# Gate projections of the attention stage: two column chunks formed together as seven half-size products

## What is computed

```
pr = split(h @ w_in)            # gates are pr[11], pr[12], pr[13]
ga, gb, gc = (sigmoid(t) for t in pr[11:14])
y = ga * (o_a @ w_proj_a) + gb * (o_b @ w_proj_b) + gc * (o_c @ w_proj_c)
return y @ w_out
# o_c = softmax(q k^T / 8) v over 768 keys, 16 query heads in 8 pairs
```

## Time and profile before

| what | value |
|---|---|
| median of three executions | 2822.43 us |
| span of the profiled execution | 2814.1 us |
| median less span (start and end around it) | 8.3 us |
| PE busy | 2697.8 us, 96% |
| DVE busy | 1246.7 us, 44% |
| ACT busy | 523.0 us, 19% |
| attention stage, first scores to last values | 753.6 to 1176.2 us |

### The profile page before, as it was taken

One profiled execution on the slowest core, in us unless ns is written; L12 is line 12 of the kernel. 1 busy time (PEld: TensorE's weight loads), 2 busy tenths in 40 slices (PEclk: granted clock), 3 DMA queues, 4 the chain that ended last, 5 costly groups with the idle time before them and its releaser, 6 DMA issues.

```text
span 2814.1 us, 32083 instructions
## 1 busy us (share of the span) xinstructions
PE 2697.8 (96%) x12682; PEld 1796.7 (64%) x12682; DVE 1246.7 (44%) x2310; ACT 523.0 (19%) x870; POOL 171.2 (6%) x140
## 2 busy tenths in 40 slices
PE   7999999999899999999799999989999999999997
PEld 3688888887544444586344333334496877888886
DVE  4255656664444344535311111146573335654644
ACT  3122121222233233211100000022322113100001
POOL 1122211220000000132000000000000000000000
PEclk9999999999999999999899999999999999999999
DMA  9622111211111111225599999942102421233330
GB/s 346 212 60 57 54 52 45 60 30 38 38 53 53 45 53 49 79 75 183 231 409 409 409 409 409 409 154 64 42 1 83 125 77 46 78 87 90 90 90 30
DMA packets 327673, 374.57 MB, mean 133 GB/s; under 512 B 10033, under 2 KB 273030, under 8 KB 324230
## 3 DMA queue, kind: packets, MB, share of 16 engines
q1 hardware_dynamic: 327286, 371.93, 38.6%
q10 hardware_dynamic: 272, 1.05, 0.1%
HBM read 370.85 MB, written 2.10 MB: 133 GB/s over the span
## 4 chain that ended last, share of the span: by engine, by line
PE 91%; DVE 4%; DVEq 1%; DMA 1%; ACT 1%; issue 1%; SPq 0%; ACTq 0%
PE psum L1650 31%; PE psum L1952 12%; PE psum L1381 8%; PE psum L2108 6%; PE psum L720 3%; PE psum L1118 2%; PE psum L1837 2%; PE psum L815 2%; PE psum L728 2%; PE psum L2642 2%; PE psum L1878 2%; PE psum L705 2%; PE psum L1308 2%; PE psum L1360 2%; PE psum L1337 1%; PE psum L2724 1%
## 5 line engine op out<-in xcount | busy, mean ns | idle before, releaser
L1650 PE MATMUL psum<-arena 128*128 128x256 f32 x4144 | 907.9, 378 | 1.0 <-ACT arena L2740 0.5
L1650 PEld LDWEIGHTS psum<-arena 128*128 128x128 f32 x4144 | 779.2, 189 | 116.2 <-issue 5.3
L1952 PE MATMUL psum<-arena 128*64 128x512 f32 x1536 | 347.6, 597 | 3.0 <-issue 2.1
L1952 PEld LDWEIGHTS psum<-arena 128*64 128x64 f32 x1536 | 104.9, 136 | 217.5 <-issue 214.4
L1381 PE MATMUL psum<-arena 128*128 128x512 f32 x512 | 233.1, 597 | 0.0
L2108 PE MATMUL psum<-arena 128*128 128x512 f32 (+1 forms) x448 | 168.1, 532 | 0.0
L1682 DVE TENSOR_TENSOR arena<-psum,arena 128x256 f32<-128x256 f32 x66 | 28.0, 425 | 315.2 <-ACT arena L1695 192.6
L1381 PEld LDWEIGHTS psum<-arena 128*128 128x128 f32 x512 | 92.4, 189 | 104.1 <-issue 104.1
L1883 DVE SCALAR_TENSOR_TENSOR arena<-psum,arena 128x512 f32<-128x512 f32 x64 | 48.0, 750 | 246.4 <-PE psum L1878 245.8
L2108 PEld LDWEIGHTS psum<-arena 128*128 128x128 f32 x448 | 84.8, 190 | 80.8 <-issue 77.3
L1657 POOL TENSOR_TENSOR arena<-arena 128x512 f32<-128x512 f32 x34 | 48.2, 1418 | 1119.7 <-DMA arena<-in_w_in 653.3
(11 more groups left out here) (378 smaller groups left out, 3202.9 us busy)
## 6 DMA issues: line engine op xcount, KB each, us to landing
arena<-in_w_gate SPq DMA_DIRECT2D x64, 1024.0 KB, 18.3
arena<-in_w_up SPq DMA_DIRECT2D x64, 1024.0 KB, 16.2
arena<-in_w_down SPq DMA_DIRECT2D x64, 1024.0 KB, 18.0
arena<-in_w_in SPq DMA_DIRECT2D x120, 512.0 KB, 4.0
arena<-in_ada_w SPq DMA_DIRECT2D x24, 1024.0 KB, 7.4
arena<-in_w_up SPq DMA_DIRECT2D x32, 512.0 KB, 5.3
arena<-in_w_down SPq DMA_DIRECT2D x32, 512.0 KB, 4.8
arena<-in_w_out SPq DMA_DIRECT2D x16, 512.0 KB, 3.8
```

Source lines behind the costliest of these rows:

```text
L1650: mm = pe.matmul(psum[:, base + b, c * HALF:(c + 1) * HALF], w, v, start=(first and q == 0 and m in (0, 2, 3, 4)), stop=(last and q == KC ...
L1952: mm = pe.matmul(psum[64 * e:64 * e + 64, bank + n, :], tokens(e, 2 * q + k), w[:, k, 512 * n:512 * n + 512], start=(q == 0 and k == 0), s ...
```

## The change

The gates of two neighbouring chunks are formed together as a pair with seven half-size products. Pair q (0 to 7) is branch a for even q, branch b for odd q, and the chunks 2(q // 2) and 2(q // 2) + 1. Every attention pair q now has one gate pair and two projections:

- step t = 0: `pe_gate` phase 0 (products 0 and 1, bank 6) and phase 1 (product 4, bank 7);
- step t = 1: phase 2 (products 3 and 5, bank 6) and phase 3 (products 6 and 2, bank 7);
- steps t = 2 and 3: `pe_branch`, the projections of the two chunks, as before but into banks 6 and 7.

Each phase's results are taken out of PSUM by `act_gate_copy` and `dve_gate`; the sigmoid is formed once per pair over 1024 columns (`act_gate`, in step t = 2), and `dve_branch` multiplies and adds. `form_gate_sums` forms the four weight sums of the next pair on DVE in step t = 3. The units of a pair are now ordered query, gate, gate, projection, projection, in the same four places. Three waits of the merge stage name the new units and counts. The core of the diff:

```diff
-        def unit_of_fill(f):
-            q, r = f // 4, f % 4
-            return 5 + 5 * q + (r + 1 if r and q < PAIRS_Q - 1 else r)
+        def unit_of_fill(q, r):
+            return 5 + 5 * q + (q < PAIRS_Q - 1) + r
...
-            return 5 * q + 1 if q else Q0
+            return 5 * q if q else Q0
...
+        def form_gate_sums(eng, q):
+
+            for e in range(2):
+                ws.arrived(eng, "attn", 0, unit_of_fill(q, e))
...
+                done(eng, "attn", 0, unit_of_fill(q - 1, 1))
+            weight_sums(eng, *gate_weights(q), gate_sums(q), "gate_sums")
+
+        PHASES = [(0, 1), (4,), (3, 5), (6, 2)]
+
+        def pe_gate(pe, q, phase):
...
+            if phase == 0:
+                for e in range(2):
+                    ws.arrived(pe, "attn", 0, u + e)
+                if q == 0:
                     pe.wait_ge(sem("head_root"), HEADS)
+                else:
+                    pe.wait_ge(sem("branch_out"), 2 * q - 1)
+            if phase == 1:
+                pe.wait_ge(sem("gate_sums"), q + 1)
...
+                    pe.wait_ge(sem("branch_out"), 2 * q)
+            if phase >= 2:
+                pe.wait_ge(sem("gate_parts"), 4 * q + phase - 1)
+            for at_, m in enumerate(PHASES[phase]):
+                for j in range(KC // 2):
+                    e, o = 2 * j, 2 * j + 1
...
+                    mm = pe.matmul(psum[:, 6 + phase % 2, at_ * HALF:(at_ + 1) * HALF], w, v, start=(at_ == 0 and j == 0),
+                                   stop=(j == KC // 2 - 1), skip_group_check=True)
...
+        def act_gate(act, q):
+
+            m = m_gate
+            act.wait_ge(sem("gate_parts"), 4 * q + 4)
+            act.activation(m, m, ACT.Exp, scale=-1.0)
...
+        def pe_branch(pe, q, e, part):
...
+            if part == 0:
+                ws.arrived(pe, "attn", 0, u)
+                pe.wait_ge(sem("gate_parts"), 4 * q + 3 + e)
...
         def dve_attn(dve):
+            form_gate_sums(dve, 0)
             for s in range(NSTEP):
                 q, t = s // 4, s % 4
+                if t == 0 and q:
+                    dve_branch(dve, q - 1, 1)
+                if t == 1:
+                    dve_gate(dve, q, 1)
+                if t == 2:
+                    dve_gate(dve, q, 3)
                 dve_max(dve, s, 0)
                 dve_max(dve, s, 1)
                 dve_scale(dve, s, 0)
...
                 turned_copy(dve, s, 1)
-                if s and s % 2 == 0:
-                    dve_fill(dve, s - 1)
+                if t == 0:
+                    dve_gate(dve, q, 0)
+                if t == 1:
+                    dve_gate(dve, q, 2)
+                if t == 3:
+                    dve_branch(dve, q, 0)
+                    if q < PAIRS_Q - 1:
+                        form_gate_sums(dve, q + 1)
...
-                    done(pool, "attn", 0, unit_of_fill(4 * KC - 3))
+                    done(pool, "attn", 0, unit_of_fill(PAIRS_Q - 2, 3))
...
-            pe.wait_ge(sem("gate_out"), FILLED)
+            pe.wait_ge(sem("branch_out"), FILLED - 1)
```

More of the change, by code:

```diff
@@ L1055, in mixed_block_kernel @@
             sources[unit_of_query(q)] = w_in_at("aq", q)
[L1056 to L1058 removed]
+        for q in range(PAIRS_Q):
+            for e in range(2):
+                c = 2 * (q // 2) + e
+                sources[unit_of_fill(q, e)] = w_in_at("g" + "ab"[q % 2], c)
+                sources[unit_of_fill(q, 2 + e)] = lambda i, b=q % 2, c=c: w_proj[b][c]
         ws.phase("attn", 1, [(sources[n],) + unit_place(4 + n % 4) for n in range(len(sources))],
@@ L1077, in mixed_block_kernel @@
         a_q = [at.take(S)]
+        gate_a, gate_u = at.take(HALF), at.take(HALF)
         at = Carve(arena, EXTRA[0], HG_END)
         a_q.append(at.take(S))
-        m_gate = [at.take(S) for _ in range(2)]
+        m_gate = at.take(2 * S)
         late = [at.take(S) for _ in range(3)]
@@ new lines, in gate_sums @@
+        def gate_sums(q):
+            if q < 4:
+                kept = [yT[:, 5 + m, :].rearrange("p (k n) -> p k n", n=P) for m in range(3)]
+            else:
+                area = Carve(arena, HG_END + NT * 2 * P, HG_END + NT * 2 * P + 2 * T)
+                kept = [area.take(KC // 2, P) for _ in range(3)]
+            return kept + [gate_weights(q)[1].rearrange("p (k h) n -> p h k n", h=2)[:, 0]]
+        def form_gate_sums(eng, q):
+            for e in range(2):
+                ws.arrived(eng, "attn", 0, unit_of_fill(q, e))
+            if q == 0:
+                eng.wait_ge(sem("head_out"), HEADS + 1)
+            elif q == 4:
+                eng.wait_ge(sem("scores_1"), 16)
+            else:
+                done(eng, "attn", 0, unit_of_fill(q - 1, 1))
+            weight_sums(eng, *gate_weights(q), gate_sums(q), "gate_sums")
@@ new lines, in mixed_block_kernel @@
+        PHASES = [(0, 1), (4,), (3, 5), (6, 2)]
+        def pe_gate(pe, q, phase):
+            u = unit_of_fill(q, 0)
+            wa, wb = gate_weights(q)
+            sums = gate_sums(q)
+            x = HT[:, :, C:T]
+            if phase == 0:
+                for e in range(2):
+                    ws.arrived(pe, "attn", 0, u + e)
+                if q == 0:
+                    pe.wait_ge(sem("head_root"), HEADS)
+                else:
+                    pe.wait_ge(sem("branch_out"), 2 * q - 1)
+            if phase == 1:
+                pe.wait_ge(sem("gate_sums"), q + 1)
+                if q == 0:
@@ L1393, in sigmoid_gate, with dve_branch @@
             act.drain()
[L1394 to L1401, removed]
+            act.activation(m, m, ACT.Exp, scale=-1.0).then_inc(sem("gate_out"), 2)
+        def pe_branch(pe, q, e, part):
+            u = unit_of_fill(q, 2 + e)
+            x = (aT, bT)[q % 2]
+            if part == 0:
+                ws.arrived(pe, "attn", 0, u)
+                pe.wait_ge(sem("gate_parts"), 4 * q + 3 + e)
+            for k in range(4 * part, 4 * part + 4):
+                mm = pe.matmul(psum[:, 6 + e, :], ws.dst("attn", u)[:, k, :], x[:, k, :], start=(k == 0), stop=(k == KC - 1))
+            if part:
+                mm.then_inc(sem("weights_used"), 1)
+        def dve_branch(dve, q, e):
+            m, c = m_gate[:, e * S:e * S + S], 2 * (q // 2) + e
+            dve.wait_ge(sem("gate_out"), 2 * q + 2)
+            done(dve, "attn", 0, unit_of_fill(q, 2 + e))
+            dve.tensor_tensor(m if q % 2 else yT[:, c, :], m, psum[:, 6 + e, :], ALU.mult)
             dve.drain()
-            if not first:
+            if q % 2:
                 dve.tensor_tensor(yT[:, c, :], yT[:, c, :], m, ALU.add)
@@ L1406, in gated_branch, with pe_filler @@
             dve.sem_inc(sem("branch_out"), 1)
[L1408 to L1414, removed]
+        def pe_filler(pe, s, part):
+            q, r = s // 4, s % 4
+            if r < 2:
+                pe_gate(pe, q, 2 * r + part)
+            else:
+                pe_branch(pe, q, r - 2, part)
         def pe_attn(pe):
```

54 lines of the change are left out of this document (41 added, 13 removed).

## The result

Four executions of the changed kernel took 2802.54 to 2809.33 us, a median of 2805.44 us against 2822.61 us for four of the kernel before: a ratio of 0.9942 with a 95% interval of 0.9929 to 0.9954. Forecast were 2809.2 us in a range of 2805 to 2815. The change is faster by 17 us, 0.6%.

A forecast was written before the change was run, and what follows sets the result against it. PE work was taken to bound the attention stage. Removed columns gave -13.2 us, all other terms 0: span 2814.1 to 2800.9, plus 8.3 to the median, 2809.2 us; range 2805 to 2815, the forecast's own 2806 to 2812.

The forecast's parts named there:

- The columns: PE in the attention stage: seven eighths of the gate columns remain, -1.65 us per pair, -13.2 us over eight pairs.
- far bound of 16.5 us: PE's largest possible gain, charging the group switch to the wide instructions: 2.06 us per pair, 16.5 us in all.
- The rule against it: Skill page on PE matmul spacing: isolated gap gives 1.65 us saved per pair, sustained spacing a loss of some 20 us.
- What had to stay hidden: Added DVE, ACT and load work around each attention pair: covered by slack at every place, taken as cost 0.
- odd pairs: DVE's weight sums at an odd pair's end delay the next softmax; 5.6 us slack before PE's transposes, cost 0.
- copy: DVE's copy of the transposes at the end of step t = 0: 0.5 us slack left, narrowest cover, cost 0.
- first step: First attention step: weight sums precede the first maximum and just fit, 0.4 us cover; bounds 0 and +1 us, 0 taken.
- The first rival: Part of the gain is given back through a new wait around DVE's queue or copy: 2813 to 2821 us, chance 0.10.
- the second: Rival: a pair's late gate-unit load blocks DVE's queue and the softmax chain; 2839 us at 21 us load, chance 0.03.
- The weight sums: Four sums on DVE at the end of a pair: 2.83 us, 2.9 with the drain, cost 0.
- the last pair: GpSimd's first merge sums beside DVE's scaling start earlier by part of a transfer: 0 to -1.3 us, 0 taken.
- the frame around the span: Whole run: the median of the runs lies 8.3 us above the profiled span, added to 2800.9 to give 2809.2 us.

The follow-up runs named there:

- `plain_pair`: Changed kernel's grouping, but each gate formed plainly with eight 512-column matmuls, no weight sums or recombination: stage 420.79 us, median 2817.36 us, ratio 0.9982 to the kernel before.
- `eighth_product`: Changed kernel plus an unread eighth half-size product of four more matmuls in phase 1: stage 421.45 us, median 2819.39 us, ratio 0.9992 to the kernel before.
- the loaded kernels: Changed kernel with extra DVE work: `sums_plus_4` (2813.49 us, once), `sums_plus_12` (2853.10 us, once) and `copy_twice` (2811.61 us, once).
- `copy_twice`: Changed kernel with DVE's copy of the transposes done twice in step t = 0: pairs 52.47 us, stage 411.72 us, total 2811.61 us, executed once.
- `sums_on_gpsimd`: Changed kernel with the weight sums formed on GpSimd instead of VectorE: stage 415.88 us, median 2816.19 us, ratio 0.9976 to the kernel before.
- `sums_plus_12`: Changed kernel with twelve more DVE adds (9.2 us) ahead of each pair's weight sums: stage 452.31 us, total 2853.10 us, executed once.
- `sums_plus_4`: Changed kernel with four more DVE adds (3.1 us) ahead of each pair's weight sums: stage 412.28 us, total 2813.49 us, executed once.

## Why the prediction was right, and where it was off

**The columns.** The sum gave -1.65 us per pair and -13.2 in all, by 0.430 and 0.216 us from start to start. Measured are 53.60 - 51.96 = 1.64 us per pair and 13.16 us between `plain_pair` and the change. Mean durations (597 and 378 ns) would have given 32 x 0.597 - 56 x 0.378 = -2.1 us per pair, a loss. The far bound of 16.5 us was wrong for the reason stated, the switch stays. One reading of it was loose: the 3.53 us of the earlier trace rows stand ahead of a group of another shape, the scores, but the 3.54 us stand behind them. Both sides of such a group cost 0.1 us, and the sum does not change by it.

**The rule against it.** The trace put the fixed cost of a narrow instruction near zero, and `eighth_product` confirmed it within 0.02 us in 13.8. Of the two figures of the Trainium skill, "TensorE: Matmul & The Clock Gate", section "Back-to-back issue gap", the isolated gap held here and the sustained spacing did not. With two passes for each instruction the first gives an estimated 3.45 us for eight wide instructions and the second 2.10; the trace has 3.44. The prediction's estimate by the first was miscalculated: with its own four passes per matmul the page's formula gives an estimated 1.58 us per pair, 12.7 in all, and not 1.65. The sum did not rest on it.

**What had to stay hidden, stayed hidden.** The tight places were named with 5.6 us (odd pairs), 0.5 us (copy) and 0.4 us (first step); the loaded kernels measured 5.6, 0.5 and 0.6 (in the first step 3.1 us added, 2.5 waited). The first rival had its place right and did not occur. The load of the gate unit never held DVE, so the second did not occur either. The weight sums took 2.84 us, forecast 2.83.

**Mis-sized: the last pair.** The term "between 0 and -1.3 us, I take 0" measured -1.48 us for the collision, a little beyond its own bound, against the profile of before that the prediction had; against its repeat, where the collision was milder, it would have been -0.4. Another 0.35 us came from the grouping, a wait that the prediction counted in its 1.6 us of idle time but gave no term. The mechanism of the collision was named, its place too; the error was to take 0 for it. The rows gave POOL's start and DVE's scaling, and a shift by part of a transfer was known to come; against DVE operations of 0.6 us a shift of one microsecond already decides between all and nothing. POOL's start moved by 2.2 us, relative to the step's scores, and all of the collision's cost was gained.

**Wrong: the frame around the span.** I took the 8.3 us between the median and the profiled span as start and end around it. The executions with both times show 1.7 to 3.7 us there; the rest was that the profiled execution was one of the shorter ones. It did no harm to the difference, but the forecast of the profiled span (2800.9, measured 2801.4) agrees for a wrong reason: the stage gained 1.8 us more than forecast, the part ahead of it 1.2 us, and the part behind it came out 3.4 us longer than in the profile of before.

**The range** of 2805 to 2815 held the median of 2805.44 only just, and the forecast's own range of 2806 to 2812 missed it. The last pair's two terms, 1.8 us together, and the open 2 us of the medians all lie on that side. The mechanism and its size in the stage are shown; that the total fell inside the range by 0.4 us is in part luck.

## What to carry to other kernels

Price a change of matmul shapes from start to start of like groups, and leave switches and idle time out of it: here that gave the gain within 1%. When work is hidden in another engine's queue, write down the slack at each place and load it once to see it. And do not move such work to an engine only because that engine looks free: here GpSimd was idle for 536 us up to the last pair, and the same sums made the stage 8.25 us longer on it, since they held up VectorE.

## What was not expected of the hardware

In these runs the longer waits of PE cost clearly more than themselves. Waits of 0.4 to 2.1 us (`copy_twice`, `sums_on_gpsimd`, even pairs of `sums_plus_12`) left the granted clock at 1.00 in the rows read and cost their own length, within 0.45 us; waits of 2.5 to 8.4 us (`sums_plus_4`, the others of `sums_plus_12`) were followed by some 3 to 6 us at 0.50, and cost 1.5 to 3.0 us on top. Nothing between 2.1 and 2.5 us was measured. A forecast of a wait on a saturated PE should carry that as a second price.
